# Spread tables of a state space stage through DRAM instead of TensorE, and a new order of page loads

## The reference: what is computed

```python
def ssd_scan(x, dt, A, B, C, h0):          # chunks of 128 tokens
    X = ch(x * dt[..., None])
    a = jnp.moveaxis(ch(dt * A), -1, 1)
    a_cum = jnp.cumsum(a, axis=-1)
    Lmat = jnp.exp(segsum(a))
    y_diag = jnp.einsum('bclhn,bcshn,bhcls,bcshp->bclhp', Cc, Bc, Lmat, X)
    decay_states = jnp.exp(a_cum[..., -1:] - a_cum)
    states = jnp.einsum('bclhn,bhcl,bclhp->bchpn', Bc, decay_states, X)
    ...
    y_off = jnp.einsum('bclhn,bchpn,bhcl->bclhp', Cc, states[:, :-1], jnp.exp(a_cum))
...
xbc, conv_state = causal_conv(xbc, conv_prev, lw['conv_w'], lw['conv_b'])
xbc = jax.nn.silu(xbc)
xs, Bm, Cm = jnp.split(xbc, (S_INNER, S_INNER + S_GROUPS * S_STATE), axis=-1)
dtv = jax.nn.softplus(dt + lw['dt_bias'])
A = -jnp.exp(lw['a_log'])
y, ssm_state = ssd_scan(xs, dtv, A, Bm, Cm, ssm_prev)
y = y + lw['d_skip'][:, None] * xs
y = rmsnorm(y * jax.nn.silu(z), lw['ssm_norm'])
```

## Time and profile before

| | us |
|---|---|
| median of the runs | 3590.25 |
| lowest run | 3589.69 |
| the profiled execution, its time | 3589.07 |
| its span, first to last instruction | 3587.3 |
| TensorE busy in the span | 3313.1 |
| vector engine busy | 2227.6 |
| GpSimd busy | 1047.8 |
| scalar engine busy | 561.3 |

### The profile page before, as it was taken

The page is one execution under the profiler, slowest core; times in us unless marked ns, Lnnn a source line. Parts: engine busy times, 40 slices in busy tenths (PEclk is TensorE's granted clock), DMA queues, the critical chain, the costliest instruction groups (busy, mean ns, idle before and its releaser), DMA issues.

```text
span 3587.3 us, 41269 instructions
## 1 busy us (share of the span) xinstructions
PE 3313.1 (92%) x15925; PEld 2840.7 (79%) x15925; DVE 2227.6 (62%) x3808; ACT 561.3 (16%) x1329; POOL 1047.8 (29%) x687
## 2 busy tenths in 40 slices
PE   8988989999898879859987799999999999999999
PEld 6865668877786667647876688899999999999988
DVE  2233655257885896688998786455555556556554
ACT  2221220212231221111557000000000000000000
POOL 0101110000331453350232232344444344444431
PEclk9998999999998988989997899999999999999999
DMA  5535675436895899884778899999999999999996
GB/s 187 184 121 211 244 257 188 159 135 231 340 406 219 344 381 357 324 355 181 301 303 315 324 359 415 364 390 395 391 391 382 395 399 392 394 390 383 386 380 255
DMA packets 220148, 1123.36 MB, mean 313 GB/s; under 512 B 24242, under 2 KB 63410, under 8 KB 109218
## 3 DMA queue, kind: packets, MB, share of 16 engines
q0 software_dynamic: 93728, 631.32, 45.1%
q1 hardware_dynamic: 123922, 473.14, 34.4%
q10 hardware_dynamic: 2304, 16.25, 1.2%
HBM read 1085.05 MB, written 35.56 MB: 312 GB/s over the span
## 4 chain that ended last, share of the span: by engine, by line
PE 72%; DVE 15%; DMA 4%; issue 3%; ACT 3%; POOL 1%; SPq 1%; DVEq 0%; POOLq 0%; ACTq 0%; another core or an unknown queue 0%
PE pj L342 24%; PE pj L2299 21%; PE pst L2266 19%; DVE wide L2214 3%; DVE gs L2202 2%; DMA gs<-in_peer_u,arena 2%; POOL gs L2252 1%; SPq L2431 1%; DVE arena L2354 1%; PE pj L1867 1%; DMA ring<-in_up 1%; ACT mix L2401 1%; PE pov L451 1%; PE pst L901 1%; DMA arena<-gates 1%
## 5 line engine op out<-in xcount | busy, mean ns | idle before, releaser
L2299 PE MATMUL pj<-arena,ring 128*128 128x248 f32 x4096 | 882.7, 375 | 26.5 <-DVE arena L2289 16.4
L2266 PE MATMUL pst<-hb,ring 128*128 128x248 f32 x4096 | 886.8, 375 | 14.0 <-DMA ring<-in_up 10.1
L2299 PEld LDWEIGHTS pj<-arena,ring 128*128 128x128 f32 x4096 | 783.3, 191 | 108.7 <-DVE arena L2289 16.8
L2266 PEld LDWEIGHTS pst<-hb,ring 128*128 128x128 f32 x4096 | 783.5, 192 | 95.5 <-DMA ring<-in_up 11.1
L2252 POOL DMA_INDIRECT gs<-in_peer_v,arena x272 | 481.9, 1772 | 928.7 <-DVE wide L2214 847.3
L2252 POOL DMA_INDIRECT gs<-in_peer_u,arena x272 | 485.2, 1784 | 875.5 <-DVE arena L2202 686.0
L2214 DVE SCALAR_TENSOR_TENSOR wide<-gs,arena,wide 128x2048 f32<-128x2048 f32 x271 | 636.7, 2350 | 60.0 <-DMA gs<-in_peer_v,arena 45.9
L2202 DVE CUSTOM_DVE_ANT_0 gs<-gs,wide 128x2048 f32<-128x2048 f32 x272 | 622.9, 2290 | 47.7 <-DMA gs<-in_peer_u,arena 29.5
L342 PE MATMUL pj<-hb,ring 128*128 128x256 f32 x2048 | 491.2, 395 | 4.4 <-DVE hb L276 3.2
L342 PEld LDWEIGHTS pj<-hb,ring 128*128 128x128 f32 x2048 | 398.8, 198 | 72.0 <-issue 14.1
L2308 DVE TENSOR_TENSOR xb<-pj,xb 128x248 f32<-128x248 f32 x256 | 105.0, 415 | 553.9 <-PE pj L2299 553.8
(11 more groups left out here) (408 smaller groups left out, 2235.9 us busy)
## 6 DMA issues: line engine op xcount, KB each, us to landing
ring<-in_w SPq DMA_DIRECT2D x160, 1024.0 KB, 5.7
ring<-in_up SPq DMA_DIRECT2D x128, 1024.0 KB, 9.2
ring<-in_down SPq DMA_DIRECT2D x256, 512.0 KB, 9.0
gates<-mix ACTq DMA_DIRECT2D x15, 1024.0 KB, 7.1
mix<-gates SPq DMA_DIRECT2D x16, 960.0 KB, 14.0
xb<-in_cache_k POOLq DMA_DIRECT2D x16, 512.0 KB, 5.8
wide<-in_cache_k POOLq DMA_DIRECT2D x16, 512.0 KB, 5.5
xb<-in_cache_v POOLq DMA_DIRECT2D x16, 512.0 KB, 7.4
```

Of the source, the lines that this page charges most:

```text
L2266: m = pe.matmul(pst[:, j % 2, 0:TD], ring[:, j % 2, c * P:(c + 1) * P], hb[:, c, XT:TA], start=(c == 0), stop=(c == DC - 1))
L2299: m = pe.matmul(sums(n), value_tile(n)[:, k * P:(k + 1) * P], wt[:, r % SLOTS * EG + k, :], start=(k == 0), stop=(k == EG - 1))
```

## The change

The spread no longer goes through TensorE and PSUM. Once per group SP stores the tables `dts` and `acs` into DRAM (`spans_d`). For each pair it then loads the two heads' rows back with a source that repeats over partitions, into one of two buffers `spans` in SBUF: dt of each head on its 64 partitions (two loads), and both heads' sums on all 128 (one load). The readers (`xd`, `xsmp`, the Exp, the gaps, the samples' decay) take them from SBUF. `broadcast` and the two scalar engine copies are gone; what `broadcast` waited for, the last pair's `mixed` and the copies of B, `turned` now waits for.

The B and C rows are spread for both groups at once, in prepare: the scalar engine picks the sample columns (`bc8`), TensorE transposes them, the scalar engine copies them and stores them into DRAM (`rows_d`), and SP loads them back onto all partitions (`rows`, four rows of 1024). `group_pe`, `group_dve` and `group_act` are gone, with `qmask` and `dtp`.

GpSimd's order changes in the first steps: key loads 4 to 6 and value load 0 stand ahead of the state store of their step, key load 7 and value load 1 behind the state load.

```diff
+        def spans_store(sp, gi):
+            cols = COLS[gi]
+            sp.wait_ge(s_dtn, 6 * gi + 5)
+            sp.dma_start(spans_d[gi, 0, :, 0:cols], dts[0:SH, 0:cols]).then_inc(s_spanned, 16)
+            sp.dma_start(spans_d[gi, 1, :, 0:cols], acs[0:SH, 0:cols]).then_inc(s_spanned, 16)
+        def spans_load(sp, gi, s):
+            S, cols = NP_ * gi + s, COLS[gi]
+            sp.wait_ge(s_spanned, 32 * gi + 32)
+            hold(sp, s_spans, 48 * S)
+            if s >= 2:
+                sp.wait_ge(s_x, S - 1)
+                sp.wait_ge(s_decay, S - 1)
+                sp.wait_ge(s_gapd, 2 * S - 2)
+                if gi == 0:
+                    sp.wait_ge(s_xTc, S - 1)
+            for e in range(2):
+                sp.dma_start(spans[e * SP_:(e + 1) * SP_, s % 2, 0, 0:cols],
+                             spans_d[gi, 0, 2 * s + e:2 * s + e + 1, 0:cols].broadcast_to([SP_, cols])).then_inc(s_spans, 16)
+            sp.dma_start(spans[:, s % 2, 1:3, 0:cols],
+                         spans_d[gi, 1, 2 * s:2 * s + 2, 0:cols][None, :, :].broadcast_to([P, 2, cols])).then_inc(s_spans, 16)
+        def rows_load(sp):
+            sp.wait_ge(s_rowd, 16)
+            sp.dma_start(rows[:, :, :], rows_d.rearrange("(k s) n -> k (s n)", s=TS)[None, :, :]
+                         .broadcast_to([P, 2 * SG, TS * SN])).then_inc(s_rowb, 16)
...
@@ prepare_pe
                     pe.wait_ge(s_dtn, 6 * gi + 6)
+                    if gi == 0:
+                        pe.wait_ge(s_rowc, 1)
+                        pe.transpose(pst[0:2 * SG * TS, 0, 0:SN], bc8, ident).then_inc(s_rowT, 1)
...
@@ prepare_act
+            if gi == 0:
+                act.wait_ge(s_silu, 4)
+                act.activation(bc8.rearrange("p (k s) -> p k s", s=TS), bc[:, :, GT:TA], ACT.Copy).then_inc(s_rowc, 1)
+                act.wait_ge(s_rowT, 1)
+                act.activation(turned8[0:2 * SG * TS, :], pst[0:2 * SG * TS, 0, 0:SN], ACT.Copy).then_inc(s_rowc, 1)
+                act.wait_ge(s_rowc, 2)
+                act.dma_start(rows_d, turned8[0:2 * SG * TS, :]).then_inc(s_rowd, 16)
...
@@ pairs_pe
             def turned():
                 pe.wait_ge(s_x, S + 1)
-                pe.wait_ge(s_decay, S + 1)
+                hold(pe, s_ymix, S)
+                pe.wait_ge(s_bctc, SG * gi + SG)
...
             quarter(0, 1)
-            if ssd:
-                broadcast()
             quarter(0, 2)
...
@@ pairs_act
-                hold(act, s_bcast, S)
-                pick = co("pair_rows")[0:SH, s:s + 1]
-                o.last(act.activation(dtp[0:SH, 0, 0:cols], dts[0:SH, 0:cols], ACT.Copy, scale=pick))
-                act.activation(dtp[0:SH, 1, 0:cols], acs[0:SH, 0:cols], ACT.Copy, scale=pick).then_inc(s_pairs, 1)
...
-                act.wait_ge(s_bcast, S + 1)
+                act.wait_ge(s_spans, 48 * S + 48)
                 hold(act, s_ymix, S)
-                act.activation(dec[:, :, :], pst[:, :, 0:GT], ACT.Exp).then_inc(s_decay, 1)
+                act.activation(dec[:, :, :], spans[:, s % 2, 1:3, 0:GT], ACT.Exp).then_inc(s_decay, 1)
...
@@ pairs_dve
             def inputs():
-                dve.wait_ge(s_bcast, S + 1)
+                dve.wait_ge(s_spans, 48 * S + 48)
                 dve.wait_ge(s_silu, CT * gi + s + 5)
+                hold(dve, s_xT, S)
...
-                dve.tensor_tensor(xd, xs[:, 0:GT], pov[:, 0:GT], ALU.mult).then_inc(s_x, 1)
+                dve.tensor_tensor(xd, xs[:, 0:GT], spans[:, s % 2, 0, 0:GT], ALU.mult).then_inc(s_x, 1)
...
             def sample_state():
                 dve.wait_ge(s_st, s * 16 + 16)
+                dve.wait_ge(s_rowb, 16)
...
@@ samples_pool
             state_load(pool, 0)
-            pages_pool(pool, "cache_k", 2)
-            pages_pool(pool, "cache_k", 3)
+            for n in range(2, 6):
+                pages_pool(pool, "cache_k", n)
             for s in range(NP_):
-                if s < 2:
-                    pages_pool(pool, "cache_k", 2 * s + 4)
-                    pages_pool(pool, "cache_k", 2 * s + 5)
-                elif s == 2:
+                if s == 0:
+                    pages_pool(pool, "cache_k", 6)
+                elif s == 1:
                     pages_pool(pool, "cache_v", 0)
-                    pages_pool(pool, "cache_v", 1)
-                elif s < 6:
+                elif 3 <= s < 6:
                     pages_pool(pool, "cache_v", 2 * s - 4)
                 state_store(pool, s)
                 if s + 1 < NP_:
                     state_load(pool, s + 1)
-                if 2 < s < 6:
+                if s == 0:
+                    pages_pool(pool, "cache_k", 7)
+                elif s == 1:
+                    pages_pool(pool, "cache_v", 1)
+                elif 3 <= s < 6:
                     pages_pool(pool, "cache_v", 2 * s - 3)
...
@@ SP, behind the load of weight tile t
+                for gi in GROUPS:
+                    pair = TILE[gi, "zx", 0, 0]
+                    if t == pair:
+                        spans_store(sp, gi)
+                    if t in (pair + 1, pair + 2):
+                        spans_load(sp, gi, t - pair - 1)
+                    if gi == 0 and t == pair + 3:
+                        rows_load(sp)
+                    if t in range(pair + 5, pair + 2 * NP_, 2):
+                        spans_load(sp, gi, (t - pair - 1) // 2)
...
@@ TensorE, and alike on the scalar and vector engines
                     pairs_pe(pe, gi, i, i < NP_, i > 0)
-                    if gi == 0 and i in (0, NP_ // 2):
-                        group_pe(pe, i // (NP_ // 2))
```

More of the change, by code:

```diff
@@ L660, in decoder_step @@
         yv = dtw
-        dtp, at = carve(at, 2, TA)
+        spans, at = carve(at, 2, 3, TA)
         cols2, at = carve(at, 2, NB, SH)
@@ L929, in prepare_pe @@
                 m.then_inc(s_bct, 1)
[L931 to L956, removed]
@@ L1031, in quarter @@
                     project(pe, gi, "zx", i, j, H[gi], 4 * n, 4 * n + 4, cols)
[L1033 to L1042, removed]
-                    pe.matmul(ptr[:, TS:2 * TS], co("pair", SH), dtp[0:SH, 1, GT:TA], start=True, stop=True)
-                pe.matmul(pst[:, 0, 0:GT], co("even", SH), dtp[0:SH, 1, 0:GT], start=True, stop=True)
-                pe.matmul(pst[:, 1, 0:GT], co("odd", SH), dtp[0:SH, 1, 0:GT], start=True, stop=True).then_inc(s_bcast, 1)
             def turned():
                 pe.wait_ge(s_x, S + 1)
-                pe.wait_ge(s_decay, S + 1)
+                hold(pe, s_ymix, S)
+                pe.wait_ge(s_bctc, SG * gi + SG)
                 for b in range(NB):
@@ L1114, in pairs_act @@
                     sample_sums_act(act)
-                act.wait_ge(s_bcast, S + 1)
+                act.wait_ge(s_spans, 48 * S + 48)
                 hold(act, s_ymix, S)
-                act.activation(dec[:, :, :], pst[:, :, 0:GT], ACT.Exp).then_inc(s_decay, 1)
+                act.activation(dec[:, :, :], spans[:, s % 2, 1:3, 0:GT], ACT.Exp).then_inc(s_decay, 1)
                 if gi == 0:
-                    act.wait_ge(s_x, S + 1)
-                    o.last(act.activation(dsmp, dsmp, ACT.Exp))
+                    for e in range(2):
+                        r = slice(e * SP_, (e + 1) * SP_)
+                        o.last(act.activation(dsmp[r, :], spans[r, s % 2, 1 + e, GT:TA], ACT.Exp))
                 act.wait_ge(s_xT, S + 1)
@@ L1156, in gaps @@
                         c = slice(b * P, (b + 1) * P)
[L1157 removed]
+                        m = dve.tensor_scalar(gap[:, e, c], spans[:, s % 2, 1 + e, c], cols2[:, 0, b, 2 * s + e:2 * s + e + 1], 0.0,
                                               ALU.subtract, ALU.min)
@@ L1204, in sample_update @@
                 dve.wait_ge(s_stn, s + 1)
-                o.step(dve.tensor_tensor(pd, st, rows[:, 1, :].rearrange("p (b n) -> p b n", n=SN), ALU.mult))
+                o.step(dve.tensor_tensor(pd, st, rows[:, SG + g, :].rearrange("p (b n) -> p b n", n=SN), ALU.mult))
                 o.step(dve.tensor_reduce(ysmp, pd, AX_X, ALU.add))
@@ L2736, in _ @@
                     o.renew()
-                    if gi == 0 and i in (0, NP_ // 2):
-                        group_act(act, i // (NP_ // 2))
                 ends_act(act, gi)
@@ L2795, in _ @@
                     o.renew()
-                    if gi == 0 and i in (0, NP_ // 2):
-                        group_dve(dve, i // (NP_ // 2))
                 ends_dve(dve, o, gi)
```

23 lines of the change are left out of this document (9 added, 14 removed).

## The result

The changed kernel takes 3570.14 us (median of 4 runs, 3565.68 to 3578.05) against 3590.25: ratio 0.9946, interval 0.9934 to 0.9958. One run of the kernel before took 15678.3 us and is left out of its median. The change is faster by about 20 us and not by the 45 forecast. The profiled execution took 3578.05 us, span 3576.4, the longest of the four.

| stretch | before | after | difference | forecast |
|---|---|---|---|---|
| start to group 0's first dt matmul | 237.2 | 236.6 | -0.6 | 0 |
| group 0: dt matmul to the end of the last L1324 (before: L1332), the sums for the norm behind the steps | 278.6 | 252.2 | **-26.4** | -42.5 |
| between the groups | 587.0 | 586.4 | -0.6 | 0 |
| group 1: dt matmul to the end of the last L1324 | 261.7 | 270.2 | **+8.5** | -2.1 |
| the rest | 2222.8 | 2231.0 | +8.2 | 0 |

The account below looks back on a forecast made before the run. Group 0 was taken to be bound by TensorE, group 1 by the vector engine and gathers. Group 0's -45.0 + 0.5 + 2 = -42.5 us and group 1's -2.1 made -44.6, so 3546 us; range 3533 to 3574.

Parts of the forecast that it names:

- part (d): Group 0, GpSimd: new order of pages and state costs nothing, but the state buffer's loop tightens; 2 us taken.
- the rival: Group 0: the state buffer's loop becomes the bound and may cost 4 to 15 us, 3548 to 3559; chance 0.12.
- `group_pe` with the slow projections: Group 0 after steps 0 and 4: gaps of 20.46 us and slow projections after them, 4.93 us, go.
- the broadcasts: Group 0: `broadcast` matmuls of 1.94 us go from the seven steps that also project, 13.6 us.
- step 3: Group 0, pages: key load 6 issued ahead of the state store removes TensorE's `cache_k` wait and slow matmuls, 5.1 us.
- The first pair's 4.2 us: Group 1: without `broadcast`, the first pair's `xd` no longer waits past the silu; it and the gathers start 4.2 us earlier.
- The gaps from SBUF: Group 1: gap subtractions read SBUF instead of PSUM, about 0.06 us each, 2.0 us in all.
- The transfers' 4.1 us: Group 1: 393 KB of added loads a pair cost 0 to 13.7 us on the DMA engines; 4.1 taken.
- "Hidden": Part (c), span loads on SP: weight tiles stand behind SP's waits, but three more lie loaded (some 30 us), so no cost.
- The loads that hold the DMA engines: Group 1: three loads per pair block the gathers, 24 us in place of 4.1 (3566), or 48 us (3590); chance 0.11.
- The stage not freed: Group 0: something the chain hides, vector engine order or a late page, takes half the gain, 3567; chance 0.04.
- Late spans: Both groups: span tables land late; eating the gain needs a 43 us landing, at 45 us 3600; chance 0.03.

Follow-up runs that it names:

- e13: Changed kernel with a second state buffer and the load of pair s + 1 issued ahead of the store of pair s: 3550.90 us, ratio 0.9882 to before.
- e12: Changed kernel with state stores, and state loads after the first, cut to 8 KB (incomplete data, no proposal): 3551.25 us, ratio 0.9893 to before.
- e7: Changed kernel with a second state buffer in the place of a row table, state and pages still on GpSimd's queue: 3564.94 us, ratio 0.9927 to before.
- e2: Changed kernel with GpSimd issuing pages and state in the order of the kernel before: 3571.61 us, ratio 0.9944 to before.
- the five kernels with the same group 1: e1, e2, e7, e12 and e13, which leave the changed kernel's group 1 alone: 3550.90 to 3571.61 us.
- e4: Changed kernel with group 1's spread loads of pairs 2 to 7 asked for two weight tiles later, same bytes: 3558.77 us, ratio 0.9909 to before.
- e1: Changed kernel with group 0's state loads and stores moved from GpSimd's queue to SP's: 3564.79 us, ratio 0.9932 to before.
- e3: Changed kernel with group 1's spread loads of pairs 2 to 7 replaced by tiny ones (incomplete data, no proposal): 3554.30 us, ratio 0.9908 to before.

## Why the prediction was wrong

The two stages came out 26.7 us above the forecast, 16.1 of them in group 0 and 10.6 in group 1.

**The step that failed is the price of the state buffer's loop**, part (d). The rows were right and the rival was named, with 0.12, but the term was 2 us and the rival's price 4 to 15. Measured against e13, where no load waits for a fresh store, it is 252.2 - 231.5 = 20.7 us (17 to 22 by the spread of the stage); with short transfers in the same loop (e12) it is gone too. A second buffer alone (e7) gave little back, since GpSimd then held the pages in its wait. Two things were wrong in how it was sized. I took the landing of the store from steps of before, at its median of 4.1 us; with the pages close ahead it is 10.0. And I let it cost in three steps, where the chain shows stores of 10.41 and 13.48 us in the first two. At the medians, 10.0 + 5.2 + 4.4 = 19.6 us, the loop would still fit into a step of 20.24; it is the late stores, up to 15.7, that made the step 23.2. That the order of pages "costs nothing" looked at when buffers come free and not at what then stands ahead of the store: the new order puts value load 0 right ahead of the second one, which in e2, with the order of before, has landed within 5 us (13.48 in after). But e2's stage is as long, because its pages come late instead. What part (d) lacked is that state and pages share GpSimd's one order of issue, in which neither had room left.

**What was removed was sized well.** Without the loop's price (e13) group 0 is 47.1 us shorter than before, against 45.0 - 0.5 = 44.5. `group_pe` with the slow projections, the broadcasts and the tail went; steps are 20.24 us, forecast 20.4. The 5.1 us of step 3 can't be told apart: the wait for `cache_k` is down to 0.8 us after the change and back at 5.3 in e2, where it makes no difference, since in after other transfers of GpSimd's are late instead.

**Group 1.** The first pair's 4.2 us came: from the dt matmul to the first gathered row behind the first pair's `xd` it took 59.81 us against 64.06. The gaps from SBUF too: a pass fell from 343 to 283 ns (medians), the 0.06 us of the forecast, and the stage without gather waits is 6.9 shorter, where 4.2 + 2.0 had been forecast. **The transfers' 4.1 us are the second term that was mis-sized**: as they stand in the change they cost 28.3 - 12.9 = 15.4, and 16.7 to 21.3 in the five kernels with the same group 1. For the same bytes at e4's place it is 3.6 to 8.7, so there the size was nearly right. "Hidden", which I wrote of SP's wait because three weight tiles lie loaded, was true for TensorE, which waits for no weight tile there, and not for the gathers, beside which the loads and the late tiles then go. Why the gathers suffer in just that moment is open: GpSimd then issues several of them back to back, but no run took that away. One reading of mine was too strong: that nothing in group 1 waits for TensorE except once. The scalar engine waits for it as well (L1122, 22.0 us in all), and nothing in the result turns on it.

**The rivals.** The loads that hold the DMA engines: 24 us by its own sum, measured 15.4 to 21.3 at the gaps and 3.6 to 8.7 at e4's place, so it was nearer the truth than the forecast, and a price per load misses that the place decides. The estimate of 31 us over the stage from the Trainium skill's table (DMA: Bandwidth & Descriptors, "Measured") lies above both. The stage not freed: its 3567 comes close to the result, but by luck; what it named, late pages, is 7.3 us of TensorE's waits in after and none in e13, so they came with the state buffer's loop. Late spans: landing 8.7 us at most, where 43 would have been needed.

## What to carry to other kernels

When a step gets shorter, look for loops through one buffer (store, load, update), price them with the transfers that will now stand ahead, at their late landings and not at the medians, and compare the sum with the new step. A second buffer, with the load issued ahead of the fresh store, removed all of the 20.7 us here. A wait in the engine that issues transfers moves everything behind it, and what leaves together afterwards can collide with a third party, as with the gathers here: ask who shares the DMA engines at that moment, not only who waits for the data. A new order of issue alone (e2) only moved the lateness between pages and state; another queue (e1) took 14 us of it away, another buffer with the order that suits it (e13) all.

## What the runs showed of the hardware

In e12 eight stores of 8 KB landed 1.6 to 10.0 us after their issue, median 7.4, most of them with 512 KB page loads under way that GpSimd had issued ahead; 8 KB loads issued after a store had landed took 1.9. The same 393 KB a pair added 3 to 21 us to the waits for gathers over the stage, by the moment at which they left and what left behind them, which I had not expected to matter at a mean DMA share of 0.94 before the change. And indirect DMA issues on GpSimd became longer with the change: in group 1's stretch up to 4.24 us, against 3.02 before. One of them starts at 1196.72, just after the gap subtractions and the multiplication behind them have begun (1195.53 to 1197.0 us). The same 4.24 us stand in e3 and e4, whose waits are about half of after's, so it is not what makes those long; no run tests what lengthens it.
